# A new order for the input LayerNorm of a decoder trunk: block 0's rows first in the load queue, statistics row by row, rows normalised by two engines, a cycle of four steps per block

## The reference

```python
def trunk(x, p0, cache_k, cache_v, page_table, states, weights):
    x = layer_norm(x, ln_in_g, ln_in_b)          # mean and variance over 1024 channels, gain, bias
    ...
    mix, st = mixer_layer(x, ...)                # starts with proj = x @ w_in: 1024 -> 9*256 columns
    x = layer_norm(ALPHA * x + mix, ln1_g[l], ln1_b[l])
    x = layer_norm(ALPHA * x + sq_relu_mlp(x, w_ff1[l], w_ff2[l]), ln2_g[l], ln2_b[l])
```

## Time and profile before

| what | value |
|---|---|
| median of three runs | 2620.07 us (2618.77 to 2621.68) |
| the profiled execution's own time | 2617.39 us |
| its span | 2615.8 us |
| PE busy | 2489.6 us, 95% of the span |
| PE weight load / DVE / ACT / POOL busy | 92% / 58% / 50% / 8% |
| chain of work that ended last, by engine | PE 88%, DVE 4%, ACT 3%, DMA 3%, issue 1%, SPq 1% |
| PE busy in 40 slices of 65.4 us | 4899999768999999999999999999999999999997 |

### The profile page before, as it was taken

The page is one execution under the profiler, slowest core; times in us unless marked ns, Lnnn a source line. Parts: engine busy times, 40 slices in busy tenths (PEclk is TensorE's granted clock), DMA queues, the critical chain, the costliest instruction groups (busy, mean ns, idle before and its releaser), DMA issues.

```text
span 2615.8 us, 37208 instructions
## 1 busy us (share of the span) xinstructions
PE 2489.6 (95%) x13647; PEld 2396.0 (92%) x13647; DVE 1525.3 (58%) x2200; ACT 1295.3 (50%) x1994; POOL 200.8 (8%) x403
## 2 busy tenths in 40 slices
PE   4899999768999999999999999999999999999997
PEld 3899999758999999999999999999988999999996
DVE  5434652165577775777775767755745665563335
ACT  4556621244565564565673555643445455344432
POOL 0001220000000000001000000000022130000001
PEclk9999999859999999999999999999999999999998
DMA  5433452332343443443433434433466565343332
GB/s 174 151 119 113 158 166 97 107 96 81 117 141 113 131 118 108 131 132 110 134 110 117 125 114 134 125 107 105 127 201 181 186 223 164 113 131 114 114 120 75
DMA packets 136066, 339.09 MB, mean 130 GB/s; under 512 B 20029, under 2 KB 63550, under 8 KB 135758
## 3 DMA queue, kind: packets, MB, share of 16 engines
q1 hardware_dynamic: 123534, 300.29, 37.2%
q0 software_dynamic: 12352, 36.42, 4.4%
HBM read 291.72 MB, written 44.92 MB: 129 GB/s over the span
## 4 chain that ended last, share of the span: by engine, by line
PE 88%; DVE 4%; ACT 3%; DMA 3%; issue 1%; SPq 1%; DVEq 0%; ACTq 0%; POOL 0%
PE PS L953 20%; PE PS L954 20%; PE PS L955 20%; PE PS L712 5%; PE PS L713 5%; PE PS L714 5%; PE PS L777 2%; PE PS L764 1%; PE PS L799 1%; PE PS L798 1%; PE PS L765 1%; PE PS L861 1%; PE PS L891 1%; DMA rows_a<-x_all 1%; PE PS L849 1%
## 5 line engine op out<-in xcount | busy, mean ns | idle before, releaser
L1240 ACT ACTIVATE w_hi<-w_raw 128x1024 fp32r<-128x1024 f32 x238 | 250.5, 1053 | 289.0 <-PE PS L955 286.5
L953 PE MATMUL PS<-a_hi,w_hi 128*128 128x416 f32 x1048 | 375.6, 358 | 5.8 <-DVE a_lo L1783 5.8
L954 PE MATMUL PS<-a_lo,w_hi 128*128 128x416 f32 x1048 | 369.1, 352 | 0.0
L955 PE MATMUL PS<-a_hi,w_lo 128*128 128x416 f32 x1048 | 368.3, 351 | 0.0
L1752 DVE TENSOR_TENSOR w_lo<-w_raw,w_hi 128x1024 fp32r<-128x1024 f32 x238 | 290.1, 1219 | 81.3 <-ACT w_hi L1240 80.9
L953 PE MATMUL PS<-h_hi,w_hi 128*128 128x416 f32 x872 | 313.3, 359 | 0.1
L954 PE MATMUL PS<-h_lo,w_hi 128*128 128x416 f32 x872 | 306.5, 351 | 0.0
L955 PE MATMUL PS<-h_hi,w_lo 128*128 128x416 f32 x872 | 305.9, 351 | 0.0
L1777 DVE TENSOR_TENSOR h_lo<-h_full,h_hi 128x416 fp32r<-128x416 f32 x160 | 94.6, 591 | 234.8 <-ACT h_hi L1253 234.7
L953 PEld LDWEIGHTS PS<-a_hi,w_hi 128*128 128x128 f32 x1048 | 199.4, 190 | 9.9 <-issue 6.2
L1240 ACT ACTIVATE w_hi_c<-w_raw 128x1024 fp32r<-128x1024 f32 x120 | 126.3, 1053 | 154.7 <-PE PS L955 154.7
(11 more groups left out here) (287 smaller groups left out, 5104.6 us busy)
## 6 DMA issues: line engine op xcount, KB each, us to landing
w_raw<-w_all SPq DMA_DIRECT2D x378, 512.0 KB, 3.7
proj_scratch<-stage SPq DMA_DIRECT2D x70, 208.0 KB, 1.9
k_rows<-kv_out SPq DMA_DIRECT2D x80, 128.0 KB, 4.1
x_scratch<-x_full SPq DMA_DIRECT2D x20, 416.0 KB, 2.6
x_residual<-x_scratch SPq DMA_DIRECT2D x5, 1664.0 KB, 8.2
pages<-ck SPq DMA_DIRECT2D x64, 128.0 KB, 2.2
pages<-ck POOLq DMA_DIRECT2D x64, 128.0 KB, 2.6
pages<-cv SPq DMA_DIRECT2D x64, 128.0 KB, 2.3
```

The costliest lines, as they stand in the source:

```text
L953: pe.matmul(out, w_h, mh_[:, k, :], start=(g == 0), stop=False)
L954: pe.matmul(out, w_h, ml_[:, k, :], start=False, stop=False)
L955: ins = pe.matmul(out, w_l, mh_[:, k, :], start=False, stop=(g == KT - 1))
L1240: act.activation(w_hi(n), raw[:, n % 2, :], ACT.Copy).then_inc(s_wh, 1)
```

## The change

It has five parts.

1. **SP**: `load_rows(0)` is issued ahead of the two constants. Behind raw weight tile 2 come the x1 stores of block 0, then weight tile 3 and `load_rows(2)`, then the small constants and weight tile 4. In the loop the stage stores and x1 stores are in the order of the new cycle, and `load_rows(b + 3)` stands behind the x1 stores of block b+1.
2. **Statistics by row**: each tile of block 0 has a semaphore of its own (`s_xr0`), and DVE waits for one tile at a time.
3. **Two engines normalise**: ACT does tiles 0 and 2, DVE tiles 1 and 3 (a `tensor_scalar` with two per-partition operands). PE waits for both.
4. **An early root**: ACT computes a square root of some elements of `ident` into `std` before it waits for any statistics.
5. **A cycle of four steps**: block b+1 is normalised at the start of block b's cycle, its transposes stand ahead of the steps p=1 and p=2, and `block_std` and `block_nmr` of a block stand directly together with its `block_norm`. `block_back(0)` comes directly behind the split of weight tile 0.

```diff
+            load_rows(0)
             const(ident[:, :], ident_d)
             const(ln_gb[:, :, :], lnp)
-            load_rows(0)
             load_raw(0)
             load_raw(1)
             load_rows(1)
             load_raw(2)
+            for k in range(0, KT, 2):
+                store_x1(0, k)
             load_raw(3)
+            load_rows(2)
             ...
+            load_raw(4)
+            for b in range(NB - 1):
                 if b:
                     store_stage(b * GRP - 1)
+                store_stage(b * GRP)
+                store_x1(b + 1, 0)
+                store_x1(b + 1, 2)
+                store_stage(b * GRP + 1)
+                if b == 0:
+                    load_raw(5)
+                store_x1(b + 1, 4)
+                store_x1(b + 1, 6)
+                if b + 3 < NB:
+                    load_rows(b + 3)
+                store_stage(b * GRP + 2)
+            store_stage((NB - 1) * GRP - 1)
@@ PE
                 if k == 0:
                     pe.wait_ge(s_nat, NR * (b + 1))
+                    pe.wait_ge(s_natv, 2 * (b + 1))
...
-                    if b + 1 < NB and p >= 2:
-                        for k in range(4 * p - 8, 4 * p - 4):
+                    if b + 1 < NB and p in (1, 2):
+                        for k in range(4 * p - 4, 4 * p):
                             turn_back(b + 1, k)
                     project(b * GRP + p)
@@ ACT
                 act.wait_ge(s_nmr, b + 1)
-                for j in range(NR):
-                    norm(x_rows(b)[0:ROW, j, :], x_rows(b)[0:ROW, j, :], j, j)
+                for j in (0, 2):
+                    row = x_rows(b)[0:ROW, j, :]
+                    act.activation(row, row, ACT.Identity, bias=nmr[0:ROW, j:j + 1], scale=rstd[0:ROW, j:j + 1]).then_inc(s_nat, 2)
...
             act.wait_ge(s_const, 32)
+            act.activation(std[0:ROW, :], ident[0:ROW, 0:NR], ACT.Sqrt).then_inc(s_root, 1)
+            wait_apart(act, s_root, 1)
             block_std(0)
             block_norm(0)
             split_hi(0)
+            block_back(0, range(KT))
             split_hi(1)
-            block_std(1)
...
+            for b in range(NB - 1):
+                j = b * GRP
                 if b:
+                    put_out(j - 1)
+                block_std(b + 1)
+                block_norm(b + 1)
                 if b == 0:
                     split_hi(2)
+                put_out(j)
+                block_back(b + 1, range(4))
+                if b == 0:
                     split_hi(3)
+                put_out(j + 1)
+                block_back(b + 1, range(4, KT))
+                put_out(j + 2)
+            put_out((NB - 1) * GRP - 1)
@@ DVE
-                dve.wait_ge(s_xin[b % 2], 16 * NR * (b // 2 + 1))
+                if b:
+                    dve.wait_ge(s_xin[b % 2], 16 * NR * (b // 2 + b % 2))
                 for j in range(NR):
+                    if b == 0:
+                        dve.wait_ge(s_xr0[j], 16)
...
+                for j in (1, 3):
+                    row = x_rows(b)[0:ROW, j, :]
+                    dve.tensor_scalar(row, row, rstd[0:ROW, j:j + 1], nmr[0:ROW, j:j + 1], ALU.mult, ALU.add).then_inc(s_natv, 1)
...
             split_lo(0)
+            block_back(0, range(KT))
             split_lo(1)
             block_var(1)
-            for b in range(NB):
-                block_back(b, range(4))
-                if b + 1 < NB:
-                    block_nmr(b + 1)
-                block_back(b, range(4, KT))
+            for b in range(NB - 1):
+                block_nmr(b + 1)
                 if b == 0:
                     split_lo(2)
+                block_back(b + 1, range(4))
+                if b == 0:
                     split_lo(3)
+                block_back(b + 1, range(4, KT))
                 if b + 2 < NB:
                     block_var(b + 2)
```

More of the change, by code:

```diff
@@ L356, in build @@
         s_ve, s_std, s_nmr = sem("var_made"), sem("std_made"), sem("nmr_made")
-        s_nat = sem("tile_normalised")
+        s_nat, s_natv = sem("tile_normalised"), sem("tile_normalised_by_vector")
+        s_root = sem("root_tried")
+        s_xr0 = [sem(f"first_rows_in{n}") for n in range(NR)]
         s_bt = sem("back_transposed")
@@ L473, in load_rows @@
                     at = b * BLK + j * ROW
-                    sp.dma_start(x_rows(b)[0:ROW, j, :], x_all[at:at + ROW]).then_inc(s_xin[b % 2], 16)
+                    sp.dma_start(x_rows(b)[0:ROW, j, :], x_all[at:at + ROW]).then_inc(s_xin[b % 2] if b else s_xr0[j], 16)
             def store_x1(b, k):
@@ L501, in _ @@
             const(bias_h[:, NH:NH + 1], sbr)
-            for b in range(NB):
-                store_x1(b, 0)
-                if b:
-                    store_stage(b * GRP - 4)
-                    store_stage(b * GRP - 3)
-                store_x1(b, 2)
-                if b:
-                    store_stage(b * GRP - 2)
-                store_x1(b, 4)
-                store_x1(b, 6)
-                if b + 2 < NB:
-                    load_rows(b + 2)
-                if b == 0:
-                    load_raw(4)
-                    load_raw(5)
+            load_raw(4)
+            for b in range(NB - 1):
                 if b:
                     store_stage(b * GRP - 1)
+                store_stage(b * GRP)
[10 more added lines that the diff above has]
+            store_stage((NB - 1) * GRP - 1)
             sp.wait_ge(s_mzero, 1)
@@ L1104, in _ @@
             split_hi(0)
+            block_back(0, range(KT))
             split_hi(1)
-            block_std(1)
-            for b in range(NB):
-                j = (b - 1) * GRP
+            for b in range(NB - 1):
+                j = b * GRP
                 if b:
-                    put_out(j)
-                    put_out(j + 1)
-                block_back(b, range(4))
-                if b:
-                    put_out(j + 2)
-                block_back(b, range(4, KT))
+                    put_out(j - 1)
+                block_std(b + 1)
+                block_norm(b + 1)
                 if b == 0:
                     split_hi(2)
+                put_out(j)
+                block_back(b + 1, range(4))
+                if b == 0:
                     split_hi(3)
-                if b + 1 < NB:
-                    block_norm(b + 1)
-                if b + 2 < NB:
-                    block_std(b + 2)
-                if b:
-                    put_out(j + 3)
+                put_out(j + 1)
+                block_back(b + 1, range(4, KT))
+                put_out(j + 2)
+            put_out((NB - 1) * GRP - 1)
             def a_act(n):
@@ L1469, in block_nmr @@
                                          op1=ALU.mult).then_inc(s_nmr, 1)
+                dve.wait_ge(s_nmr, b + 1)
+                for j in (1, 3):
+                    row = x_rows(b)[0:ROW, j, :]
+                    dve.tensor_scalar(row, row, rstd[0:ROW, j:j + 1], nmr[0:ROW, j:j + 1], ALU.mult, ALU.add).then_inc(s_natv, 1)
             def block_back(b, ks):
```

## The result

The changed kernel took 2595.95 us (median of 4 runs, 2595.41 to 2596.68) and the kernel before, run beside it, 2620.32 us (4 runs, 2618.77 to 2621.68). The ratio is 0.9907, with a 95% interval of 0.989 to 0.9925. The prediction was 2597.5, with a range of 2592 to 2604. The profiled execution took 2596.68 with a span of 2594.7, against 2617.39 and 2615.8 before: 20.7 us between the two (21.1 of span), while the medians differ by 24.4. The profiled run of before lay 2.93 under its median and that of the changed kernel 0.73 over its own: 20.71 + 2.93 + 0.73 = 24.37.

What follows compares the result with a forecast made beforehand. PE's four waits (23.7 us) for copies held up by ACT's list were taken as the bound. Block 1's transposes at 42.3 plus 97.5 plus 2.0 slow start end at 141.8, not 164.67: 22.9 us less, forecast 2597.5, range 2592 to 2604.

Steps and rivals of the forecast that it cites:

- What bounds the kernel, and the sum: PE's waits before 164.67 us bound it; the 20 steps end at 141.8, saving 22.9 us, for 2597.5.
- Part 1: Start, rows ahead of constants, statistics by row: statistics from 12.3 instead of 12.44 us, bounds -0.9 and +1.2.
- the second rival: Start: block 0's rows land before the constants, so tile-by-tile statistics work; 1 to 3 us more gain, 2595.5; chance 6%.
- Part 2: Early root on ACT: the 1.28 us table load moves into idle time; block 0's rows begin at 18.8 instead of 20.20.
- Part 3: Normalisation on two engines: ACT's two rows 2.3 us, DVE's 2.2 beside them; PE's first transposes at 21.2 instead of 24.98.
- Part 4: Block 0's copies ahead: store wait 1.7 us, block 0 done at 32.2, PE waits about 9 until block 1's transposes at 42.3.
- Part 5: Cycle from 42.3 us: 19 steps and 8 transpose sets, 97.5, plus 2.0 slow start, no wait between; end at 141.8.
- Spare (a): ACT in each cycle: copy out, root and rows take 3.8 us against PE's step of 4.53, leaving 0.7 spare.
- Spare (c): Row loads in each cycle: block b+3's rows land at 5.7 of the next cycle, asked for at 15.4; 9.7 us spare.
- Small waits in each cycle: Rival: PE idles 0.3 to 1.8 us before transposes of blocks 2, 3 and 4; 6 us less gain, 2603; chance 10%.
- Time given back behind the steps: Rival: part of the 22.9 us returns behind 164.67, where something hangs on a transfer; 2608, or 2620 for all; chance 5%.
- Rows late: Rival: row loads share a denser queue and land late in every cycle; a landing time of 32 us gives 2630; chance 3%.

Runs made afterwards that it cites:

- e11: Kernel before, with ACT's root and DVE's reciprocal of a block moved to directly ahead of its rows, nothing else: 2606.73 us, ratio 0.9953.
- e4: Changed kernel with all four tiles of block 0 awaited before the first statistics: 2594.33 us, ratio 0.9911 to the kernel before.
- e1: Changed kernel with the two constants issued ahead of block 0's rows again, statistics still by tile: 2592.7 us, ratio 0.9908 to the kernel before.
- e3: Changed kernel without the early root: 2596.8 us, ratio 0.9923 to the kernel before.
- e7: Changed kernel with the first two x1 stores issued ahead of weight tile 2: 2594.58 us, ratio 0.9915 to the kernel before.
- e2: Changed kernel with ACT normalising all four tiles of a block and DVE none: 2605.97 us, ratio 0.9962 to the kernel before.
- e5: Changed kernel with constants first, one wait for all tiles, no early root, ACT normalising all four tiles: 2608.36 us, ratio 0.9964 to the kernel before.
- e6: Kernel before with rows first, statistics by row, early root and two engines normalising, old lists from there on: 2617.87 us, ratio 1.0003.
- e9: Changed kernel with constants first, two x1 stores ahead of weight tile 2, transposes ahead of p=2 and p=3: 2587.47 us, ratio 0.988 to before.
- e12: Changed kernel run again unchanged: 2596.01 us, ratio 0.9914 to the kernel before.

## Why the prediction came right, step by step

- *What bounds the kernel, and the sum.* Right as to the place: the end of the 20 steps moved from 164.78 to 143.22 with PE unbroken in the cycle, and the part behind it stayed. The end was forecast at 141.8, 1.4 too early, and nearly all of that is there at T1 (part 4 below). With it and the 0.5 us behind the steps the same working gives 2597.2 + 1.4 + 0.5 = 2599.1. That the time came out 3 us below this, within 1.6 us of the forecast, is luck: the working carried over that the median lies 2.7 above the profiled run, which was 2.9 for the kernel before but -0.7 for the changed one.
- *The cause named for PE's waits*, "because ACT's list holds a root for rows still in flight", was half of it. e11 takes away just that (the root, and with it the reciprocal on DVE) and gains 10.7 of the 21.6 us; then DVE's list, with statistics ahead of ready copies, becomes the wait. And the cause doesn't fit the first of the four waits: behind the wait of 6.63, ACT's root of block 1 waited 7.04 us for statistics that DVE ran from 28.09 on, behind a weight split and without a wait for a transfer:

```profile
33.77 0.20 ACT L1070 ACTIVATE std<-var 104x4 f32<-104x4 f32 x1 [7.04 <-DVE var L1459]
```

The forecast didn't suffer, since the new order puts block 0's copies ahead of these statistics and moves root and statistics of the later blocks.
- *Part 1.* Right in sign and size: the cast at 12.26 (I had 12.0) and statistics at 12.40 (12.3), all eight together, and e4 shows that waiting by tile is worth nothing. The queue shows in the DMA issues from 0 to 40 us (name, queue, KB, us to landing): `ident` took 9.2 us to land behind the rows, where before, ahead of them, it took 1.8:

```profile
ident<-ident_d SPq DMA_DIRECT2D x1, 64.0 KB, 9.2
```

The Trainium skill (DMA: Bandwidth & Descriptors, "Queues, rings and completion order"), cited in the prediction, says that each DMA engine takes its descriptors in ring order; the 9.2 us agree, as does e1. What failed is the second rival's price: I gave tile-by-tile statistics 1 to 3 us, and e1 measures 4.0 to 4.3, because the store wasn't later there (4.4 us from issue to landing, against 4.7).
- *Part 2.* Right: 18.86 for the first rows, forecast 18.8, and e3 finds 1.2 to 1.8 us at T1.
- *Part 3.* ACT's two rows 2.37 (2.3), transposes at 21.34 (21.2). DVE's row was mis-sized: 0.81 us, not 1.08, within the range of 0.54 to 1.21; the second starts 0.73 behind the first, so both take 1.53 (forecast 2.2). It changed nothing, ACT being the longer of the two.
- *Part 4.* The wait for the first store was 2.49, forecast 1.7 (it ended with a landing at 28.97, forecast 28.0). Block 1's statistics started at 34.77, forecast 33.4, and T1 was 43.65, forecast 42.3. Of these 1.35 us, 0.8 are the store wait (e7 shows what it was made of), 0.2 the copies of block 0, and 0.3 the split of weight 1, for which DVE waited 0.36 us; 0.1 were there at T0. The upper bound of 3.7 for the store wait comes to 3.3 by its own terms (23.3 + 3.7 + 2.6 - 26.3). The one wait on PE was 9.49 (about 9).
- *Part 5.* 99.57 from T1, forecast 97.5 + 2.0 = 99.5. Repeats show 99.6 to 101.0 for the same work, so the slow start is 2.1 to 3.5 rather than 2.0, and the bound of 3.0 was too low. Spare (a), forecast 0.7, was 0.77; e2 shows how near the edge that is: 2.3 us more of row work gave waits of 1.3 to 1.9 in each of three blocks. Spare (c) held: DVE waited for no rows in the cycle.
- *Rivals.* Small waits in each cycle: not there, but exactly what e2 and e5 bring. Time given back behind the steps: 0.5 of 21.6, of the size of the spread of that part. Rows late: no wait for a DMA in the cycle. What no rival covered is that the parts don't add: parts 1 to 3 alone give 0 (e6), parts 4 and 5 alone 9.6 of some 24 us (e5), and both together all of it.

Left open: why the medians of before and after differ by about 3 us more than their profiles, also on the chip of e9 to e12 (2620.01 - 2596.01 = 24.0). The granted clock of the whole run goes with it: of the 40 runs of before made beside the experiments, those at 0.979 had spans of 2613.6 to 2616.1 us, those at 0.974 or 0.975 spans of 2618.3 to 2621.9. The profiled one had 0.977, and no profile of a slower run of before was taken, so where its clock is lower isn't shown.

## What to carry to other kernels

When an engine with an in-order list waits, look at what stands ahead in the list of the engine that it waits for, and then look for the same pattern in the next engine's list before costing the gain: taking the root out of ACT's way alone gave half (e11). When a second engine takes a share of a piece of work, look at what that share stands ahead of in its own list: DVE's two rows gave 0 in the old order, between two halves of the copies, and 10 us in the new one. What sets a period can change from one block to the next, so each is to be read by itself (e6). Small constants that an early instruction needs go ahead of large loads in the queue, and a wait by tile pays only then (4 us here).

## What the runs showed of the hardware that I had not expected

- DVE's scale and shift of a 104x1024 fp32 row in place took 0.81 us (ten of them, 0.806 to 0.814), and 0.542 for 104x512: twice the elements cost 1.5 times as much.
- The time at the lower clock behind a wait of 8.7 to 9.5 us differed between profiles of one and the same kernel, by 1.4 us of PE's time (7.62 and 9.02 us from block 1's first transposes to its second, mean granted clock 0.78 and 0.65).
- `ident`, 64 KB queued behind 1.7 MB of rows, took 9.2 us to land against 1.8 ahead of them; the constants held DVE and ACT until 12.26.
